# Small vectors on ScalarE's queue, router weights later, conv states in 96 partitions, and a query job ahead of the key norms

## The chip, the cores and the metric

The kernel runs on one core of a Trainium2 chip. The number that counts is the device time of one execution in microseconds (us). The core has a matrix engine (TensorE, here PE, with its weight loads PEld), a vector engine (VectorE, DVE), an activation engine (ScalarE, ACT), GpSimd (POOL) and SyncE (SP), which here only issues DMAs. Any of SP, ACT and POOL can issue a DMA; the profile calls these issues SPq, ACTq and POOLq.

## What is computed

One layer of a decoder trunk for a prompt of 256 tokens and 8 samples of one token each, 264 tokens in all, everything in float32:

```python
mod = jax.nn.silu(c) @ w['w_mod'] + w['b_mod']
h = rms_norm(x, w['g_norm1']) * (1 + sc1) + sh1
proj = h @ w['w_in']
q, k, v, fl, z, xbc, dtr, ga, gb = split_cols(proj, IN_SIZES)
q = rms_norm(q, w['g_q']);  k = rms_norm(k, w['g_k'])
logf = jax.nn.log_sigmoid(fl + w['b_f'])
o_att = forgetting_attention(...)      # adds the cumulated logf to the scores
xa = concat([conv0, xbc])              # conv0: 3 past columns per sample, 3072 channels
y_ssm = mamba2_branch(z, xbc, dt=softplus(dtr + dt_bias), a=-exp(a_log), d_skip, ...)
m = sigmoid(ga) * (o_att @ w_pa) + sigmoid(gb) * (y_ssm @ w_pb);  x += gt1 * (m @ w_o)
h2 = rms_norm(x, w['g_norm2']) * (1 + sc2) + sh2
x += gt2 * moe(h2)                     # router h2 @ w_router + b_router, 16 experts, 2 per token
```

## The kernel before

Activations lie transposed, features on the 128 partitions and the 264 tokens along the free axis, in eight blocks (KD). The work is a list of **jobs**, written out by hand at the start of `build`. Each engine's program walks the same list, and a job takes the next of seven PSUM banks in turn (`bank_of`). TensorE fills a bank, and ACT or DVE reads it out (`release`) and frees it with a semaphore. So the order of the list is the order of every engine's instructions. The first jobs are these:

- `cT` and `xt`: the condition and x are transposed on TensorE (`flip`, L1566).
- `vecs`: the vectors `vrow` are transposed. `ssq`: the sum of squares of x (L1603).
- `mod 1`, `modt 1`: the scale columns of the modulation (L1587, then two transposes). DVE then scales x (`normed`, L1120 to L1126).
- `cst 0`, `cst 1`: the conv states `csin` are transposed, 24 pieces of 24 x 128 (L1608), and DVE copies them to `stT` (L1201).
- `mod 0`, `modt 0`: the shift columns. DVE adds them for the samples (L1187, semaphore `h_samples`), and ACT adds them for the prompt, block after block (`shifted`, L846, semaphore `h_ready`).
- `fd`: dt and forget logits, eight matmuls with `w_forget_dt` (L1614). A long row of small DVE and ACT steps on `fd` follows.
- `k 0` to `k 3` (L1633) and `q 0` (L1629); `ft`: transposes of the head columns. It needs the end of the `fd` steps.
- `kn 0` to `kn 3` (L1636): sums of squares of the keys within a head. They need one DVE product of all four key blocks (L1254). ACT then takes four square roots (L897), DVE one reciprocal (L1258) and one scaling (L1260).
- `q 1` to `q 4`, `qn 0` to `qn 3` (the same four steps for queries 0 to 3), `q 5` to `q 7`, `v 0`, `qn 4` to `qn 7`, `v 1` to `v 3`. Then come attention, the Mamba branch, the merge, the router and the experts.

SP issues the weight slabs (1 MB each) in the order of use. There are six ring slots, and a slab goes out when the last job that read its slot has filled its bank. Two of the eight slabs of `mod 1` and `mod 0` lie in other tiles (`att_T`, `conv_out`). Between the last of those eight and the first input slab (the keys') SP runs `load_small`: two DMAs for `w_forget_dt`, one for the router's weights, and nine that put single floats onto partitions or one short row (g_q and g_k twice, dt_bias, b_f, a_log, d_skip, b_router). All twelve count on one semaphore, `late_in` (its name on the chip is small_weights_landed). TensorE waits for all twelve ahead of `fd`, and so does DVE. ACT issues the early loads: the conditions, x, the vectors of `vrow` with conv_w last, the conv states and the page table.

At the end SP streams the experts' weights in halves of 1 MB (L558) through 18 buffers, each released by TensorE.

## Time and profile before

| what | value |
|---|---|
| median of 3 runs | 831.83 us (828.68 to 833.68) |
| the profiled execution | 828.73 us |
| its span, first to last instruction | 827.1 us |
| TensorE busy | 768.6 us, 93% of the span |
| DVE, ACT, POOL busy | 365.9, 304.8, 95.4 us |
| DMA | 219.67 MB, 266 GB/s on the mean |

The profile shows one execution. Times of instructions are counted from the span's start. A row of the timeline has the start, the length, the engine, the line and the operation, and in brackets how long the engine had been idle before it and what the profile takes for the releaser. That releaser is inferred. Where the named engine had been done for long, something else released the wait. "PEclk" is the granted clock of TensorE as a share of full speed.

### The profile page before, as it was taken

What the parts mean: (1) busy time and instruction counts of PE and PEld (TensorE: products, weight loads), DVE (VectorE), ACT (ScalarE), POOL (GpSimd) and SP (SyncE); (2) the same over time, 40 slices, a digit from 0 to 9 for tenths busy, and PEclk for the clock granted to TensorE, in tenths of its full rate; (3) what the DMA queues carried; (4) which work ended last, traced back from release to release, by engine and by line L of the source; (5) the groups of instructions that cost most, each with busy time, mean ns of one, the idle gap of its engine ahead of it and who ended that gap; (6) DMA issues with size and microseconds to landing.
All of it is one profiled execution on the core that took longest, in us unless ns stands there. A gap on an engine that the chain in (4) does not pass through costs nothing.

```text
span 827.1 us, 12505 instructions
## 1 busy us (share of the span) xinstructions
PE 768.6 (93%) x4573; PEld 533.5 (64%) x4573; DVE 365.9 (44%) x847; ACT 304.8 (37%) x733; POOL 95.4 (12%) x156
## 2 busy tenths in 40 slices
PE   3798999999998999889999999999599999999997
PEld 3475787778776677679878788888343444344434
DVE  2455467777771373585998310122311133122213
ACT  1212247657763382646875001012221122122213
POOL 3321012112102105211111100000000000000000
PEclk9999999999999999999999989999689999999999
DMA  9797455969866323139998986353869999999992
GB/s 282 245 355 215 140 182 157 328 219 331 279 219 200 111 66 103 55 105 355 360 288 269 333 333 203 103 216 134 323 236 420 420 422 420 422 421 420 423 417 94
DMA packets 93531, 219.67 MB, mean 266 GB/s; under 512 B 11792, under 2 KB 67672, under 8 KB 78980
## 3 DMA queue, kind: packets, MB, share of 16 engines
q1 hardware_dynamic: 78850, 181.71, 60.3%
q0 software_dynamic: 7984, 31.87, 11.8%
q10 hardware_dynamic: 6634, 5.25, 2.0%
q8 instruction: 39, 0.64, 0.3%
q14 instruction: 24, 0.20, 0.1%
HBM read 207.58 MB, written 13.22 MB: 267 GB/s over the span
## 4 chain that ended last, share of the span: by engine, by line
PE 61%; DMA 12%; ACT 9%; DVE 6%; SPq 5%; issue 4%; POOL 1%; ACTq 1%; POOLq 1%; DVEq 0%
PE bank L1633 13%; PE bank L1943 9%; PE bank L1864 7%; SPq L558 5%; PE bank L1965 5%; PE bank L1566 4%; DMA out_ssm_sample<-arena 4%; PE bank L1629 4%; PE bank L1872 4%; DMA arena<-in_w_down 3%; PE bank L1846 3%; PE bank L1984 2%; PE bank L1587 2%; DMA arena<-in_conv_w 2%; DVE conv_work L1298 1%
## 5 line engine op out<-in xcount | busy, mean ns | idle before, releaser
L1633 PE MATMUL bank<-h_normed,weight_ring 128*128 128x264 f32 x1024 | 240.6, 392 | 4.4 <-ACT conv_work L998 2.0
L1633 PEld LDWEIGHTS bank<-h_normed,weight_ring 128*128 128x128 f32 x1024 | 193.6, 192 | 40.8 <-issue 3.5
L1943 PE MATMUL bank<-arena,h_normed 128*64 128x512 f32 x176 | 79.6, 607 | 0.0
L1864 PE MATMUL bank<-y_T,weight_ring 128*128 128x264 f32 x256 | 60.1, 399 | 0.2 <-DVE y_T L1412 0.2
L1943 PE MATMUL bank<-weight_ring,h_normed 128*64 128x512 f32 x192 | 56.3, 594 | 0.6 <-ACT h_normed L1040 0.6
L1864 PEld LDWEIGHTS bank<-y_T,weight_ring 128*128 128x128 f32 x256 | 50.4, 198 | 9.3 <-issue 0.3
L1492 DVE TENSOR_TENSOR arena<-arena,bank 128x512 f32<-128x512 f32 x8 | 8.8, 1098 | 105.0 <-PE bank L1943 105.0
L1499 DVE SCALAR_TENSOR_TENSOR x_residual<-bank,modulation,x_residual 128x256 f32<-128x256 f32 x64 | 28.8, 484 | 57.8 <-PE bank L1984 57.8
L1566 PE MATMUL bank<-identity,arena 128*128 128x128 f32 (+5 forms) x236 | 32.4, 279 | 15.5 <-ACT arena L839 9.4
L1566 PEld LDWEIGHTS bank<-identity,arena 128*128 128x128 f32 (+5 forms) x236 | 27.1, 150 | 26.1 <-issue 11.4
L990 ACT ACTIVATE arena<-conv_out,expanded 128x128 f32<-128x128 f32 x128 | 38.3, 388 | 11.2 <-DVE arena L1375 10.4
L1943 PEld LDWEIGHTS bank<-weight_ring,h_normed 128*64 128x64 f32 x192 | 17.5, 137 | 35.9 <-issue 34.8
L1040 ACT ACTIVATE h_normed<-bank,conv_tails 128x128 f32<-128x128 f32 x64 | 17.4, 382 | 60.8 <-PE bank L1566 60.8
L1965 PE MATMUL bank<-arena 128*64 128x512 f32 x88 | 39.2, 594 | 0.0
L1298 DVE SCALAR_TENSOR_TENSOR conv_work<-conv_work,vectors 128x288 f32<-128x288 f32 x72 | 37.5, 521 | 2.5
L808 POOL DMA_INDIRECT h_normed<-h_scratch,token_rows x8 | 8.1, 1010 | 264.8 <-DVE token_rows L1460 144.0
L1943 PEld LDWEIGHTS bank<-arena,h_normed 128*64 128x64 f32 x176 | 24.2, 140 | 13.8 <-issue 13.8
L1943 PE MATMUL bank<-conv_out,h_normed 128*64 128x512 f32 x64 | 30.6, 631 | 0.3 <-ACT h_normed L1040 0.3
L1872 PE MATMUL bank<-arena,weight_ring 128*128 128x264 f32 x128 | 30.2, 391 | 0.0
L1629 PE MATMUL bank<-h_normed,weight_ring 128*64 128x264 f32 x256 | 30.2, 397 | 0.0
L1984 PE MATMUL bank<-arena,conv_out 128*128 128x264 f32 x128 | 29.9, 387 | 0.0
L1846 PE MATMUL bank<-att_T,weight_ring 128*128 128x264 f32 x128 | 28.9, 387 | 0.0
(359 smaller groups left out, 1191.9 us busy)
## 6 DMA issues: line engine op xcount, KB each, us to landing
weight_ring<-in_w_in SPq DMA_DIRECT2D x36, 1024.0 KB, 5.9
weight_ring<-in_w_mod SPq DMA_DIRECT2D x22, 1024.0 KB, 9.8
arena<-in_w_up SPq DMA_DIRECT2D x14, 1024.0 KB, 19.9
weight_ring<-in_w_gate SPq DMA_DIRECT2D x14, 1024.0 KB, 19.9
arena<-in_w_down SPq DMA_DIRECT2D x11, 1024.0 KB, 26.3
weight_ring<-in_w_up SPq DMA_DIRECT2D x10, 1024.0 KB, 18.5
arena<-in_state_ssm POOLq DMA_DIRECT2D x8, 1024.0 KB, 8.8
out_ssm_sample<-arena POOLq DMA_DIRECT2D x8, 1024.0 KB, 9.7
```

What stands on the lines that cost most here:

```text
L558: sp.dma_start(half[s], (wg, wu, wdn)[kind][2 * j + e][:, 2048 * h:2048 * h + 2048]).then_inc(moe_full[s // 2], 16)
L990: ins = fn(bx[:, NST * c:NST * c + NST], bc[:, b, 0, :], ACT.Copy, scale=xdt[:, c, b:b + 1])
L1298: link(v.scalar_tensor_tensor(acc, x[:, w:w + XO], vec[:, 104 + 24 * w + i:105 + 24 * w + i], acc, ALU.mult, ALU.add), conv_ready if w == ...
L1566: return tr(out, x, ident[0:k, 0:k])
L1629: ins = mm(ps[64 * x:64 * x + 64, 0:T], slot(s)[:, c, o:o + HD], hT[:, c, :], start=c == 0, stop=c == KD - 1, tile_position=(0, 64 * x))
L1633: ins = mm(ps[:, 0:T], w, hT[:, c, :], start=c == 0, stop=c == KD - 1)
L1846: ins = mm(ps[:, 0:T], slot(s)[:, c, 128 * (i % 2):128 * (i % 2) + 128], attT[:, c, :], start=c == 0, stop=c == KD - 1)
L1864: ins = mm(ps[:, 0:T], w, yT[:, c, :], start=c == 0, stop=c == NXB - 1)
L1872: ins = mm(ps[:, 0:T], slot(s)[:, c, 128 * (i % 2):128 * (i % 2) + 128], gT[:, c, :], start=c == 0, stop=c == KD - 1)
L1943: ins = mm(banks[i][BLK * e:BLK * e + BLK, :], xg[:, 4 * h + c, BLK * e:BLK * e + BLK], ws[e][:, c, :], start=h == 0 and c == 0, stop=h == ...
L1965: ins = mm(banks[2 + q][BLK * e:BLK * e + BLK, :], aT[:, 2 * h + c, BLK * e:BLK * e + BLK], ws[e][:, c, 512 * q:512 * q + 512], start=h == ...
L1984: mm(comb_bank(c)[:, 0:T], outs[:, 128 * c:128 * c + 128], selT[:, j % 2, :], start=True, stop=True)\
```

## The change

Four edits. (1) The nine small DMAs leave SP's program for ACT's, behind the Silu of the conditions, and count on a semaphore of their own (`head_in`). TensorE's `fd` waits for the two weight DMAs only. DVE's first step on `fd` and ACT's Exp of a_log wait for `head_in`. (2) The router's weights are issued by SP four input slabs later, on a third semaphore. The router's first job `sw` waits for it. (3) The conv states are loaded as 96 rows of 768 floats in place of 24 rows of 3072. TensorE makes 6 transposes of 96 x 128 of them in place of 24, and DVE makes 6 copies of 96 elements with a stride in place of 2 copies of 288. (4) The job `q 1` stands ahead of `kn 0`.

```diff
-        csin = ar[:, D:D + CD]
+        csin = ar[0:96, D:D + CD // 4]
...
-        jobs += [("k", i) for i in range(4)] + [("q", 0)] + [("ft",)] + [("kn", i) for i in range(4)]
-        jobs += [("q", i) for i in range(1, 5)] + [("qn", i) for i in range(4)]
+        jobs += [("k", i) for i in range(4)] + [("q", 0), ("ft",), ("q", 1)] + [("kn", i) for i in range(4)]
+        jobs += [("q", i) for i in range(2, 5)] + [("qn", i) for i in range(4)]
...
-                sp.dma_start(wr[:], t["w_router"].rearrange("(k p) e -> p k e", p=128)).then_inc(late_in, 16)
-                for h in range(2):
-                    sp.dma_start(gqk[64 * h:64 * h + 64, 0:1], t["g_q"].rearrange("o d -> d o")).then_inc(late_in, 16)
...
+                if s == loads[loads.index(("in", COL_K)) + 4]:
+                    sp.dma_start(wr[:], t["w_router"].rearrange("(k p) e -> p k e", p=128)).then_inc(router_in, 16)
...
-            act.dma_start(csin[0:24, :], t["state_conv"].rearrange("o b w c -> (o b w) c")).then_inc(st_in, 16)
+            act.dma_start(csin, t["state_conv"].rearrange("o b w (q c) -> (o b w q) c", q=4)).then_inc(st_in, 16)
...
             link(fn(crow[0:NC, :], crow[0:NC, :], ACT.Silu), cond_ready)
+            for h in range(2):
+                act.dma_start(gqk[64 * h:64 * h + 64, 0:1], t["g_q"].rearrange("o d -> d o")).then_inc(head_in, 16)
...
                     link(fn(fdw[:, 0, :], fd[:], ACT.Abs))
+                    act.wait_ge(head_in, 16 * 9)
...
-                    release(dve, v.tensor_copy(stT[:, 12 * j[1]:12 * j[1] + 12, :],
-                                               ps[:, 0:288].rearrange("p (c s) -> p c s", c=12)), j)
+                    st4 = stT[:].rearrange("p (q c) s -> p c s q", q=4)
+                    for c in range(3):
+                        ins = v.tensor_copy(st4[:, 3 * j[1] + c], ps[:, 96 * c:96 * c + 96].rearrange("p (s q) -> p s q", q=4))
+                    release(dve, ins, j)
...
-                    for q in range(12):
-                        c = 12 * j[1] + q
-                        ins = flip(ps[:, 24 * q:24 * q + 24], csin[0:24, 128 * c:128 * c + 128])
+                    for q in range(3):
+                        c = 3 * j[1] + q
+                        ins = flip(ps[:, 96 * q:96 * q + 96], csin[:, 128 * c:128 * c + 128])
                 elif k == "fd":
-                    pe.wait_ge(late_in, 16 * 12)
+                    pe.wait_ge(late_in, 32)
...
                 elif k == "sw":
+                    pe.wait_ge(router_in, 16)
+                    pe.wait_ge(head_in, 16 * 9)
```

SP's issues between the last modulation slab and the sixth input slab, with what each waits for; before:

```order
L597 DMA conv_out<-in_w_mod 128x2x1024
L538 DMA w_forget_dt<-in_w_in 128x8x32
L539 DMA w_forget_dt<-in_w_in 128x8x16
L540 DMA w_router_sb<-in_w_router 128x8x16
L542 DMA qk_gain<-in_g_q 64x1
...
L548 DMA router_bias<-in_b_router 1x16
L599 DMA weight_ring<-in_w_in 128x8x256 [waits bank_filled2] x4
L599 DMA weight_ring<-in_w_in 128x8x256 [waits bank_filled6] x2
```

and after the change:

```order
L592 DMA conv_out<-in_w_mod 128x2x1024
L540 DMA w_forget_dt<-in_w_in 128x8x32
L541 DMA w_forget_dt<-in_w_in 128x8x16
L594 DMA weight_ring<-in_w_in 128x8x256 [waits bank_filled2] x4
L583 DMA w_router_sb<-in_w_router 128x8x16
L594 DMA weight_ring<-in_w_in 128x8x256 [waits bank_filled6] x2
```

The key slab follows the two weight DMAs at once, and the router's weights stand behind four slabs.

TensorE from the first query job to the first query norm, with bank waits, before (L1629 is a query job, L1636 a norm):

```order
L1566 MATMUL bank<-identity,head_work 128x32 x3
L1636 MATMUL bank<-conv_out,head_blocks 128x264 [waits qk_squared,bank_read1]
L1636 MATMUL bank<-conv_out,head_blocks 128x264 [waits qk_squared,bank_read2]
L1636 MATMUL bank<-conv_out,head_blocks 128x264 [waits qk_squared,bank_read3]
L1636 MATMUL bank<-conv_out,head_blocks 128x264 [waits qk_squared,bank_read4]
L1629 MATMUL bank<-h_normed,weight_ring 64x264 [waits slot_full2,bank_read5]
L1629 MATMUL bank<-h_normed,weight_ring 64x264 x15
```

and after (L1635 is a query job, L1642 a norm):

```order
L1572 MATMUL bank<-identity,head_work 128x32 x3
L1635 MATMUL bank<-h_normed,weight_ring 64x264 [waits slot_full2,bank_read1]
L1635 MATMUL bank<-h_normed,weight_ring 64x264 x15
L1642 MATMUL bank<-conv_out,head_blocks 128x264 [waits qk_squared,bank_read2]
L1642 MATMUL bank<-conv_out,head_blocks 128x264 [waits qk_squared,bank_read3]
L1642 MATMUL bank<-conv_out,head_blocks 128x264 [waits qk_squared,bank_read4]
L1642 MATMUL bank<-conv_out,head_blocks 128x264 [waits qk_squared,bank_read5]
```

The query job has moved in front of the four key norms, and three query jobs are left between them and the query norms.

ScalarE at the same place, before:

```order
L890 DMA out_logf_sample<-logf_tok 8x16
L897 ACT_TABLE_LOAD
L897 ACTIVATE conv_work<-bank1,eps_col 128x264 [waits bank_filled1]
L897 ACTIVATE conv_work<-bank2,eps_col 128x264 [waits bank_filled2,bank_read1]
```

and after:

```order
L894 DMA out_logf_sample<-logf_tok 8x16
L897 ACTIVATE arena<-bank 128x264 [waits bank_filled1]
L901 ACT_TABLE_LOAD [waits bank_filled2]
L901 ACTIVATE conv_work<-bank,eps_col 128x264 [waits bank_read1]
L901 ACTIVATE conv_work<-bank,eps_col 128x264 [waits bank_filled3,bank_read2]
```

The load of the square root's table waited for nothing before. Now it stands behind the wait for the first key norm's bank.

## Rows read from the trace of the kernel before

**Rows 1.** Section 1 of the page: busy time, share of the span, instructions.

```profile
PE 768.6 (93%) x4573; PEld 533.5 (64%) x4573; DVE 365.9 (44%) x847; ACT 304.8 (37%) x733; POOL 95.4 (12%) x156
```

**Rows 2.** Timeline of all engines, 11 to 59 us: start, length, instruction, idle before.

```profile
11.56 17.53 SPq L539 DMA_DIRECT2D w_forget_dt<-in_w_in  x1
...
24.70 1.28 ACT L868 ACT_TABLE_LOAD   x1 [15.49 <-issue]
...
29.14 3.94 SPq L540 DMA_DIRECT2D w_router_sb<-in_w_router  x1
...
33.12 0.60 SPq L542 DMA_DIRECT2D qk_gain<-in_g_q  x1
...
33.80 0.95 DVE L1201 COPY conv_states<-bank 128x288 f32<-128x288 f32 x2
...
35.12 0.41 PE L1566 MATMUL bank<-identity,mod_rows 128*128 128x128 f32 x2 [0.66 <-ACT mod_rows L865]
...
35.64 0.42 DVE L1176 TENSOR_TENSOR modulation<-bank,vectors 128x36 f32<-128x36 f32 x2 [0.89 <-PE bank L1566]
...
36.41 3.30 ACT L846 ACTIVATE h_normed<-conv_out,modulation 128x256 f32<-128x256 f32 x8 [1.43 <-DVE h_normed L1187]
...
37.69 0.32 SPq L548 DMA_DIRECT2D router_bias<-in_b_router  x1
...
38.95 5.42 PE L1614 MATMUL bank<-h_normed,w_forget_dt 128*48 128x264 f32 x16 [3.42 <-ACT h_normed L846]
...
44.30 14.51 PE L1633 MATMUL bank<-h_normed,weight_ring 128*128 128x264 f32 x64
```

**Rows 3.** Windows: bounds, length, busy of each engine, granted clock, DMA share, GB/s.

```profile
16.00:20.00 4.00, 3.37 (x18) 2.80 (x17) 3.57 (x10) 0.00 (x0) 0.00 (x0) 1.00 1.00 190
...
36.00:38.50 2.50, 0.00 (x0) 0.00 (x0) 0.29 (x2) 2.09 (x6) 1.06 (x2) 1.00 0.12 7
...
39.60:43.20 3.60, 3.60 (x10) 1.69 (x9) 0.00 (x0) 0.11 (x1) 1.51 (x3) 0.53 1.04 341
...
67.00:70.50 3.50, 3.50 (x16) 1.71 (x16) 1.51 (x1) 1.40 (x3) 0.00 (x0) 0.51 1.10 333
...
130.00:136.00 6.00, 5.98 (x42) 4.93 (x43) 4.97 (x13) 2.71 (x6) 0.96 (x2) 1.00 0.31 87
...
431.30:435.00 3.70, 3.69 (x11) 2.91 (x12) 3.70 (x4) 3.66 (x9) 0.71 (x2) 0.63 1.12 221
620.00:800.00 180.00, 178.28 (x858) 75.89 (x856) 39.92 (x109) 37.85 (x126) 5.95 (x6) 1.00 1.01 421
```

**Rows 4.** Timeline of all engines, 59 to 86 us.

```profile
58.84 3.86 SPq L599 DMA_DIRECT2D weight_ring<-in_w_in  x1
...
59.09 0.33 ACTq L878 DMA_DIRECT2D cf_scratch<-cums  x1
...
64.32 1.26 DVE L1254 TENSOR_TENSOR conv_out<-arena 128x1056 f32<-128x1056 f32 x1
...
64.93 1.28 ACT L897 ACT_TABLE_LOAD   x1 [1.27 <-DVE logf_tok L1243]
...
65.72 2.56 PE L1636 MATMUL bank<-conv_out,head_blocks 128*128 128x264 f32 x8 [2.48 <-DVE conv_out L1254]
...
68.21 15.55 PE L1629 MATMUL bank<-h_normed,weight_ring 128*64 128x264 f32 x128
...
68.99 6.75 DVE L1258 RECIPROCAL conv_work<-conv_work 128x1056 f32<-128x1056 f32 x1 [3.42 <-ACT conv_work L897]
...
83.70 2.05 PE L1636 MATMUL bank<-conv_out,head_blocks 128*128 128x264 f32 x8
```

**Rows 5.** Timeline of TensorE at two later idle times.

```profile
130.02 0.88 PE L1673 MATMUL bank<-arena 128*64 128x128 f32 x12 [1.34 <-ACT arena L913]
...
431.31 12.63 PE L1633 MATMUL bank<-h_normed,weight_ring 128*128 128x264 f32 x48 [1.97 <-ACT conv_work L998]
```

**Rows 6.** Waits of SP over the whole span: waiter, releaser, total us, times, longest.

```profile
SPq L558 <- PE bank L1943: 75.5, 21, 14.8
```

More of the change, by code:

```diff
@@ L353, in build @@
         st_in = sem("conv_states_landed")
-        late_in = sem("small_weights_landed")
+        late_in = sem("head_weights_landed")
+        head_in = sem("head_vectors_landed")
+        router_in = sem("router_weights_landed")
         pt_in = sem("page_table_landed")
@@ L539, in load_small @@
                 sp.dma_start(wfd[:, :, SH:HB], win[:, :, COL_F:COL_F + NH]).then_inc(late_in, 16)
-                sp.dma_start(wr[:], t["w_router"].rearrange("(k p) e -> p k e", p=128)).then_inc(late_in, 16)
-                for h in range(2):
-                    sp.dma_start(gqk[64 * h:64 * h + 64, 0:1], t["g_q"].rearrange("o d -> d o")).then_inc(late_in, 16)
-                    sp.dma_start(gqk[64 * h:64 * h + 64, 1:2], t["g_k"].rearrange("o d -> d o")).then_inc(late_in, 16)
-                sp.dma_start(hcol[0:SH, 0:1], t["dt_bias"].rearrange("o d -> d o")).then_inc(late_in, 16)
-                sp.dma_start(hcol[SH:HB, 0:1], t["b_f"].rearrange("o d -> d o")).then_inc(late_in, 16)
-                sp.dma_start(hcol[0:SH, 1:2], t["a_log"].rearrange("o d -> d o")).then_inc(late_in, 16)
-                sp.dma_start(hcol[0:SH, 2:3], t["d_skip"].rearrange("o d -> d o")).then_inc(late_in, 16)
-                sp.dma_start(brow[:], t["b_router"].rearrange("(o d) -> o d", o=1)).then_inc(late_in, 16)
             def states_stored(i):
@@ L839, in _ @@
             link(fn(crow[0:NC, :], crow[0:NC, :], ACT.Silu), cond_ready)
+            for h in range(2):
+                act.dma_start(gqk[64 * h:64 * h + 64, 0:1], t["g_q"].rearrange("o d -> d o")).then_inc(head_in, 16)
+                act.dma_start(gqk[64 * h:64 * h + 64, 1:2], t["g_k"].rearrange("o d -> d o")).then_inc(head_in, 16)
+            act.dma_start(hcol[0:SH, 0:1], t["dt_bias"].rearrange("o d -> d o")).then_inc(head_in, 16)
+            act.dma_start(hcol[SH:HB, 0:1], t["b_f"].rearrange("o d -> d o")).then_inc(head_in, 16)
+            act.dma_start(hcol[0:SH, 1:2], t["a_log"].rearrange("o d -> d o")).then_inc(head_in, 16)
+            act.dma_start(hcol[0:SH, 2:3], t["d_skip"].rearrange("o d -> d o")).then_inc(head_in, 16)
+            act.dma_start(brow[:], t["b_router"].rearrange("(o d) -> o d", o=1)).then_inc(head_in, 16)
             def shifted():
@@ L1200, in _ @@
                     ps = filled(dve, j)
-                    release(dve, v.tensor_copy(stT[:, 12 * j[1]:12 * j[1] + 12, :],
-                                               ps[:, 0:288].rearrange("p (c s) -> p c s", c=12)), j)
+                    st4 = stT[:].rearrange("p (q c) s -> p c s q", q=4)
+                    for c in range(3):
+                        ins = v.tensor_copy(st4[:, 3 * j[1] + c], ps[:, 96 * c:96 * c + 96].rearrange("p (s q) -> p s q", q=4))
+                    release(dve, ins, j)
                 elif k == "fd":
                     ps = filled(dve, j)
-                    dve.wait_ge(late_in, 16 * 12)
+                    dve.wait_ge(head_in, 16 * 9)
                     w0, w1, w2 = fdw[:, 0, :], fdw[:, 1, :], fdw[:, 2, :]
```

## The prediction

> **What bounds the kernel now.** The page's busy list comes first: TensorE is busy for 768.6 of 827.1 us, 93% [rows 1]. Nothing else is near that. So the end moves only if TensorE's idle time or its slow stretches shrink, and the reader should look for these at the places that the diff touches. Both are in the first 90 us. The timeline shows TensorE idle for 3.42 us ahead of the `fd` matmuls, and `fd` takes 5.42 us [rows 2]. It is idle for 2.48 us ahead of the key norms [rows 4]. The windows add that both gaps are followed by a slow stretch: from 39.6 to 43.2 us the granted clock was 0.53, from 67.0 to 70.5 us 0.51, that is, close to the lower of its two levels, 1.2 GHz in place of 2.4 [rows 3].
>
> **Who holds up `fd`.** The row names ACT's L846 as the releaser [rows 2]. I don't believe it. `fd`'s first matmul needs the first of ACT's eight blocks only. They start at 36.41 us and take 3.30 us together, 0.41 each, so the first was there at 36.82, and the matmul starts at 38.95, 2.1 us later. What else it waits for are the twelve DMAs of `load_small`. The first of the nine vectors was issued at 33.12 and the last at 37.69, done at 38.01, 0.9 us ahead of the matmul [rows 2]. In the stretch from 36 to 38.5 us the DMA engines moved 7 GB/s [rows 3]: they wait for issues, not for bytes. The cost is SP's, 4.9 us for nine issues one after another, and the key slab stands behind them.
>
> **Edit 1, the vectors on ACT's queue.** ACT has room: it was idle for 15.49 us before its table load at 24.70 [rows 2], so from 9.2. Nine issues at SP's pace end at 14.1, and nothing there waits for ACT. `fd` then needs the two weight DMAs and ACT's first block. The weight DMAs are in the queue by 29.09, when SP turns to the next issue [rows 2]; I take them as landed by 36, since from there on only those 7 GB/s moved [rows 3]. So `fd` starts at 36.82 plus a little, 36.9: **2.05 us gained**. The key slab is now issued from 29.1 on. The router's DMA needed 3.94 us for its issue in that place, so the slab may be in the queue at 33.1. In the trace the slab was used without an idle time at 44.30, at most 6.3 us after its issue at 38.05 [rows 2]. That puts it at 39.4 at the latest, and `fd` ends at 40.6 or later: covered, with 1.2 us to spare. ACT's and DVE's new waits for `head_in` stand where the old one stood on DVE, and behind the Abs on ACT. Their data are on the way 20 us earlier, so I cost them at nothing.
>
> **The clock in `fd`.** The slow stretch cost 3.6 us x (1 - 0.53) = 1.7 us [rows 3]. The idle time ahead of it shrinks from 3.42 to 36.9 - 35.53 = 1.4 us, with 0.66 us just before it, on the other side of two transposes [rows 2]. Two rows lie on either side: 1.34 us of idle at 130.02 left the clock at 1.00, and 1.97 us at 431.31 was followed by 0.63 [rows 3, 5]. 1.4 plus 0.66 lies between them, so I take half, **0.85 us**, with 0 and 1.7 as the ends.
>
> **Edit 3, conv states in 96 partitions.** On TensorE 24 transposes become 6, ahead of `mod 0`. This can bring at most what DVE leaves. DVE's copies start at 33.80 and the modulation's add at 35.64 [rows 2]. Two copies of 288 elements took 0.95 us and two operations of 36 elements 0.42 [rows 2], so a copy of 96 should take some 0.27 and six of them 1.6 us. They end at 35.4, before the add's 35.64. So nothing is lost, and at most 0.2 is gained. If the stride makes each copy as dear as one of 288, they end at 36.7 and `fd` starts 1.05 later: the low end of this term. I take 0.
>
> A rule bears on this edit. From 16 to 20 us the DMA engines are full and move only 190 GB/s, against 421 in the experts' stretch [rows 3]; this is where the conv states are on the way. The Trainium skill, page "SBUF — State Buffer", on the DMA port swizzle, says that partitions reach SBUF over 16 ports by some bits of their number, so that 24 partitions use six of them and 96 all. By that rule the full rate comes back there and the modulation's slabs land up to 2 us earlier. The sum would gain no more than the 0.2 us above, since DVE is next.
>
> **Edit 2, the router's weights.** They are first used some 430 us later, in `sw`. Their DMA now goes ahead of the fifth input slab, which waits for `mod 0` anyway. Nothing, unless that slab becomes late. It serves `q 4`, over 30 us on.
>
> **Edit 4, `q 1` ahead of the key norms.** Before: idle from 63.24 to 65.72, and a slow stretch that cost 3.5 x (1 - 0.51) = 1.7 us, of which 2.56 - 2.05 = 0.5 lies in the norms and 1.2 in the four query jobs behind (15.55 us, so 3.6 each at full clock) [rows 3, 4]. After: `q 1` runs from 63.24 to 66.85. The keys' product ended at 65.58 [rows 4], so the norms follow at once, until 68.9. Three query jobs last until 79.7, where before the query norms started at 83.70. But a new wait is due there. ACT's table load stood ahead of the norms' wait, at 64.93 [rows 4]. Now it stands behind the first norm. From the norms' start to the reciprocal it took 68.99 - 65.72 = 3.27 us; with the table's 1.28 added and the clock's 0.5 taken off, the reciprocal starts at 66.85 + 4.05 = 70.9 and ends at 77.65 (6.75 us). Scaling (1.3, as the product of equal size) ends at 78.95, the queries' product (1.26) and its signal at 80.35. TensorE waits for some 0.7 us, and **3.3 us are gained** (83.70 - 80.35). Later steps keep their distances.
>
> **Does it reach the end?** SP waits for TensorE's expert matmuls 21 times, 75.5 us in all [rows 6]. So the experts' stream is released by TensorE's progress, although it runs at 421 GB/s from 620 to 800 us [rows 3]. It starts earlier by what TensorE gains.
>
> **The sum.** 2.05 + 0.85 + 0 + 3.3 = 6.2 us. The profiled execution took 828.73 us (span 827.1, 1.6 around it), which gives 822.5. It lies 3.1 below the median of the runs shown, 831.83; the median is what will be compared, so the forecast is 831.83 - 6.2 = **825.6 us**. The ends of the terms (1.0 to 2.25, 0 to 1.7, 2.5 to 4.0) give gains of 3.5 to 8.0, so 823.8 to 828.3.
>
> **Rivals.**
> - *The vectors were not what held up `fd`.* The profile names ACT, and the sixth block ends near 38.9. Then `fd` stays where it is, and 3.3 us remain: 828.5. Against it: no instruction of TensorE waits for the sixth block there.
> - *The gap moves to the query norms.* If the chain over ACT and DVE is 2.5 us longer than I make it, edit 4 brings 0.8, and the sum is 3.7: 828.1. For it: the table load behind the wait; against: the rest of the chain has rows.
> - *The gain is lost downstream.* If the experts' stream had a start of its own, the end would not move: 831.8. The stream's full 421 GB/s speaks for it, SP's waits against.
> - *Slower: ACT's issues are held behind SP's.* SP's second weight DMA held its issue for 17.53 us, until 29.09 [rows 2]. If ACT's nine stand behind that, they end at 29.1 + 4.9 = 34.0, and the root behind them, due at 24.70, comes 9.3 us late. Less some 2 us of slack on DVE, `fd` starts at 44.1, 5.2 later than before; less the 3.3 of edit 4, the time is some 2 us up: 834. It decides from about 33 us on: until then the other gains cover the hold. Against it: at 59.09 ACT issued a DMA in 0.33 us, inside an issue of SP that was held for 3.86 [rows 4].
>
> The Trainium skill's page "DMA: Bandwidth & Descriptors" (Queues, rings and completion order) says that SP and ACT have rings of their own but no descriptor generator of their own, which leaves that rival open; its section "Issuing engines are not separate DMA queues" says that a second issuing engine saves issue time only. Issue time is what the rows show to be short.
>
> **Chances.** Forecast 0.60; vectors not the cause 0.12; gap moves 0.10; lost downstream 0.10; slower 0.08. About 0.5%, 4.2 us, is what a measurement can tell from no change. Below 827.7 lie most of the forecast's cases and a few of the second and third rival's: faster 0.60. Slower than 836 needs the last rival with more than its price, or a slab that comes late, and medians of a kernel whose runs spread over 5 us: 0.07. The rest, 0.33, is the same. The range takes in the forecast's own ends, spread by some 2 us, and the three rivals without a slowdown: 822 to 832.
>
> **What would show it.** Right: in the trace of after, `fd` starts within 0.2 us of ACT's first block; the idle time ahead of it is under 2 us; no idle time ahead of the key norms and a clock of 1.00 behind them; 0.3 to 1.2 us idle ahead of the query norms; every later landmark some 6 us earlier. Wrong: `fd` at or after 38.5; ACT issues of more than 1 us each; a wait for the key slab; DVE's copies past 35.6; an end that keeps its time while the start of the attention moves.

## The result

The changed kernel takes **824.86 us** (median of 11 runs, 822.07 to 828.33), the kernel before 829.92 (11 runs beside it, 828.68 to 833.68): ratio 0.9938, 95% interval [0.9917, 0.9958]. That is 5.1 us less, 0.6%; 825.6 was forecast. Two later measurements of the same kernel say that this was probably a lucky sample: 828.11 against 830.04, ratio 0.9980 [0.9954, 1.0007], and 827.38 against 829.55, ratio 0.9982 [0.9951, 1.0013]. Neither of the two can be told from no change by itself. The median of all 35 runs is 826.3. The kernel before, timed against itself, gave 829.53, ratio 1.0003 [0.9977, 1.0030]. So the gain is some 3.5 us, with single runs of either kernel spread over 10. The second median and that of edit 1 below each take in one slow execution, more than 1.5% above the kernel's fastest (834.61 and 836.80), which the ratios leave out; without it they are 827.72 and 826.49.

The profiled execution of the changed kernel took 828.33 us (span 826.8 against 827.1 before); it is the slowest of its 11. Its page, busy time of each engine (compare [rows 1]):

```profile
PE 767.7 (93%) x4555; PEld 530.6 (64%) x4555; DVE 365.6 (44%) x851; ACT 304.5 (37%) x733; POOL 95.6 (12%) x156
```

These sums show nothing of the change. The timeline of all engines from 9 to 46 us shows what the page doesn't (start, length, instruction, idle time before; compare [rows 2]):

```profile
9.33 0.54 ACTq L836 DMA_DIRECT2D qk_gain<-in_g_q  x1
...
11.62 15.37 SPq L541 DMA_DIRECT2D w_forget_dt<-in_w_in  x1
...
13.88 0.30 ACTq L842 DMA_DIRECT2D router_bias<-in_b_router  x1
14.28 1.28 ACT L871 ACT_TABLE_LOAD   x1 [4.97 <-issue]
...
27.03 8.76 SPq L594 DMA_DIRECT2D weight_ring<-in_w_in  x4
...
31.45 1.07 PE L1593 MATMUL bank<-conv_out,cond_T 128*32 128x256 f32 x16 [0.45 <-DMA conv_out<-in_w_mod]
...
32.31 1.33 DVE L1207 COPY conv_states<-bank 128x96 f32<-128x96 f32 x6
...
33.70 0.43 DVE L1180 TENSOR_TENSOR modulation<-bank,vectors 128x36 f32<-128x36 f32 x2
...
34.46 3.30 ACT L849 ACTIVATE h_normed<-conv_out,modulation 128x256 f32<-128x256 f32 x8 [1.43 <-DVE h_normed L1191]
35.12 5.42 PE L1620 MATMUL bank<-h_normed,w_forget_dt 128*48 128x264 f32 x16 [1.53 <-ACT h_normed L849]
```

ACT's nine issues end at 14.18, none held. `fd` starts 0.66 us after ACT's first block begins (0.41 for the block and a signal), at 35.12 in place of 38.95. The idle time ahead of it fell from 3.42 to 1.53 us, and yet `fd` takes 5.42 us as before: the windows show the granted clock low behind it again (columns as in [rows 3]):

```profile
32.00:34.00 2.00, 0.93 (x14) 0.24 (x6) 1.81 (x10) 0.38 (x1) 0.83 (x2) 1.00 0.98 333
34.00:36.00 2.00, 0.88 (x3) 0.44 (x4) 0.35 (x2) 1.54 (x4) 0.78 (x2) 0.79 1.11 337
36.00:38.00 2.00, 2.00 (x6) 0.98 (x5) 0.00 (x0) 1.76 (x5) 0.54 (x1) 0.50 1.11 336
```

The timeline from 54 to 92 us, all engines (compare [rows 4]):

```profile
59.33 3.78 PE L1635 MATMUL bank<-h_normed,weight_ring 128*64 128x264 f32 x32
...
63.04 2.05 PE L1642 MATMUL bank<-conv_out,head_blocks 128*128 128x264 f32 x8
63.16 0.39 ACT L897 ACTIVATE arena<-bank 128x264 f32<-128x264 f32 x1 [3.48 <-PE bank L1635]
63.84 1.28 ACT L901 ACT_TABLE_LOAD   x1 [0.29 <-PE bank L1642]
...
67.28 6.75 DVE L1264 RECIPROCAL conv_work<-conv_work 128x1056 f32<-128x1056 f32 x1 [5.54 <-ACT conv_work L901]
...
76.83 2.02 PE L1642 MATMUL bank<-conv_out,head_blocks 128*128 128x264 f32 x8 [0.91 <-DVE conv_out L1260]
```

`q 1` (59.33) fills the gap, the key norms (63.04) follow without an idle time and at full clock, and the wait that was forecast ahead of the query norms is there, 0.91 us. The query norms start at 76.83, 6.87 us before the old 83.70.

**Where the lead went.** The table gives the lead, in us, over the first profile of the kernel before: how much earlier the same instructions of all engines start (median over a stretch of 15 us that begins at the time given). Positive is earlier; "end" is the difference of the spans. The kernels under the first four rows are explained below. Every profile of this study stands in the table.

```
profile                  90    330    345    375    420    450    690   end
changed, first         6.90   7.03   5.76   7.39   0.93   1.11   0.37   0.4
changed, second        5.25   4.48   4.70   4.74   4.74   3.89   4.63   2.4
changed, third         5.72   3.71   3.23   4.86  -1.25  -1.07  -0.25  -0.9
before, second         0.33   0.82   0.83   0.83   0.83   0.65   0.10   0.0
edit 1 alone           1.61   1.62   3.31   3.31   3.31   3.20   3.44   3.1
edit 4 alone           2.61   2.97   2.97   2.97   2.97   1.50   2.73   2.3
edit 3 alone           2.20   2.47   2.47   2.47   1.79  -0.19  -0.16  -1.9
four small packets     1.25   1.30   1.54   1.58   0.99  -0.10   1.45   1.4
split semaphore       -0.58  -0.71   0.97   2.59  -3.09  -4.20  -3.43  -3.8
+ table load           5.36   5.11   4.60   6.23  -0.25  -0.08   0.89  -1.0
+ filler matmuls       7.73   3.81   3.93   3.94   3.94   1.11   3.85   3.8
+ stores on GpSimd     7.18   7.04   8.73  10.36  10.36   8.10   5.55   2.7
+ all three            9.69  10.23   9.53  11.15  11.15   9.27  12.05  11.5
```

A lead of 5.3 to 6.9 us leaves the first 90 us of the changed kernel, as the forecast said, and from 600 to 815 us any lead is carried on, within 0.5 us. In the first and the third profile it is lost between 375 and 420 us: 6.5 and 6.1 us, 1.6 of which had only just come from matmuls at full clock (345 to 375 us). ACT's queue shows where. Timeline of ACT in the first profile:

```profile
371.09 0.39 ACTq L974 DMA_DIRECT2D out_ssm_prompt<-arena  x1
372.25 0.60 ACT L973 ACTIVATE arena<-bank 128x512 f32<-128x512 f32 x1 [1.19 <-PE bank L1798]
372.88 7.09 ACTq L974 DMA_DIRECT2D out_ssm_prompt<-arena  x1
380.09 4.20 ACT L994 ACTIVATE arena<-conv_out,expanded 128x128 f32<-128x128 f32 x14 [7.25 <-issue]
```

and in the second, where the lead was kept:

```profile
373.74 0.39 ACTq L974 DMA_DIRECT2D out_ssm_prompt<-arena  x1
374.90 0.60 ACT L973 ACTIVATE arena<-bank 128x512 f32<-128x512 f32 x1 [1.19 <-PE bank L1798]
375.53 0.61 ACTq L974 DMA_DIRECT2D out_ssm_prompt<-arena  x1
376.26 4.78 ACT L994 ACTIVATE arena<-conv_out,expanded 128x128 f32<-128x128 f32 x16 [0.76 <-ACT arena L973]
```

The fourth store of the prompt's final states was held for 7.09 us on ACT's queue, and the products for the sample states (L994), which VectorE's chain waits for, stand behind it. The chain of work that leads to 421 us in the first profile runs through that issue:

```profile
372.88 7.09 ACTq L974
...
382.15 2.73 ACT arena L994 x9
...
384.91 1.28 DVE arena L1381
```

### The profile page after: what moved, and what is told of

Same layout as the page of the kernel before. It is cut to its first block, busy times and chain, and to the rows that moved or that the text cites. A ratio compares the mean times of both kernels' runs of the same rounds, so it can differ in the third digit from the quotient of the medians.

```text
span 826.8 us, 12475 instructions
## 1 busy us (share of the span) xinstructions
PE 767.7 (93%) x4555; PEld 530.6 (64%) x4555; DVE 365.6 (44%) x851; ACT 304.5 (37%) x733; POOL 95.6 (12%) x156
## 4 chain that ended last, share of the span: by engine, by line
PE 65%; DVE 11%; ACT 8%; DMA 6%; issue 4%; SPq 2%; ACTq 1%; POOL 1%; POOLq 1%; DVEq 0%
PE bank L1639 14%; PE bank L1951 11%; PE bank L1872 7%; PE bank L1973 6%; PE bank L1572 4%; PE bank L1880 4%; DMA arena<-in_w_down 3%; PE bank L1854 3%; PE bank L1992 3%; PE bank L1635 2%; DVE arena L1381 2%; SPq L551 2%; PE bank L1593 2%; DVE arena L1385 2%; DMA arena<-in_x_sample 1%
## 5 line engine op out<-in xcount | busy, mean ns | idle before, releaser
L994 ACT ACTIVATE arena<-conv_out,expanded 128x128 f32<-128x128 f32 x128 | 38.3, 388 | 17.5 <-DVE arena L1381 10.2
L1635 PE MATMUL bank<-h_normed,weight_ring 128*64 128x264 f32 x256 | 29.4, 388 | 0.0
## 6 DMA issues: line engine op xcount, KB each, us to landing
arena<-in_w_up SPq DMA_DIRECT2D x14, 1024.0 KB, 19.9
```

The source lines that it names most:

```text
L994: ins = fn(bx[:, NST * c:NST * c + NST], bc[:, b, 0, :], ACT.Copy, scale=xdt[:, c, b:b + 1])
L1635: ins = mm(ps[64 * x:64 * x + 64, 0:T], slot(s)[:, c, o:o + HD], hT[:, c, :], start=c == 0, stop=c == KD - 1, tile_position=(0, 64 * x))
```

## The experiments

**The changed kernel, unedited, twice.**

> The changed kernel once more, for a second profiled execution. My reading of the first pair of traces: the change is 3.8 us ahead at the start of fd, 6.9 us ahead at the end of the first query norms, 5.8 us ahead at the ssm_prompt products, and only 1.1 us ahead at the start of the pa jobs, because one DMA issue of ScalarE was held for 7.09 us there. Theory A (the hold is an accident of that execution): this trace has no such hold, and keeps 4 us or more of its lead up to the pa jobs; end near 824. Theory B (the hold comes with the change, since the stores meet SP's slabs 6 us earlier): it is here again, and the lead at the pa jobs is again under 2 us. The fast sum of squares (3.80 us against 5.52 before) should be the clock's state at the start and not the change: it may be here or not.

> The changed kernel once more, unedited. It had 824.9 and 828.1 us in two measurements, against 829.9 and 830.0 for the kernel before, and single edits 826.8 to 828.5. A third decides between a gain of 5 and one of 2: if the landmarks are right (7.0 and 4.5 us of lead at 330 us, less what the held store takes in some executions), 825 to 827. In its trace: fd starts within 0.3 us of ScalarE's first block, 0.9 us of idle ahead of the query norms, and a held fourth store only if the first store comes within 0.2 us of the state load.

Times above. In the second profile `fd` starts at 35.48 and takes 6.71 us, in the third at 36.29 and takes 5.42. Each stands behind 2.15 us of idle time, in place of 1.53: VectorE's six copies end 0.7 us behind the transposes there, and the modulation's add waits for them. This happens where the statistics' matmuls (`ssq`) took 5.07 and 5.49 us; in the first profile they took 3.80. These matmuls vary like that in every kernel of this study (the kernel before 5.52 and 5.36, edit 1 alone 3.80), so it isn't the change. In the third profile the trace has the clock at 0.50 from 19.8 to 23.2 us, in the others with long `ssq` matmuls at 1.00, so why is open. In the profiles with long `ssq` matmuls TensorE doesn't wait for the last modulation slab at all. What it gains there is the time of the conv states' transposes, 6 in place of 24: from the transposes of `modt 1` to the first matmul of `mod 0` it takes 0.84 us in the changed kernel's third profile, in place of 1.94. Before, then after:

```profile
28.87 0.41 PE L1566 MATMUL bank<-identity,mod_rows 128*128 128x128 f32 x2 [0.66 <-ACT mod_rows L865]
...
30.81 1.93 PE L1587 MATMUL bank<-weight_ring,cond_T 128*32 128x256 f32 x32
```

```profile
28.57 0.41 PE L1572 MATMUL bank<-identity,mod_rows 128*128 128x128 f32 x2 [0.66 <-ACT mod_rows L868]
...
29.41 1.93 PE L1593 MATMUL bank<-weight_ring,cond_T 128*32 128x256 f32 x32
```

The 0.91 us of idle time ahead of the query norms is there in all three. In the second profile the fourth store isn't held (0.61 us), so the hold doesn't come with the change each time. In the third profile the fourth store is held again, 6.74 us, with the first store 0.11 us after the state load, as expected.

**The kernel before, unedited.**

> The kernel before, unedited, as a measure of what time and trace do by themselves. Time 829 to 830.5. In its trace fd starts 0.9 to 1.0 us after the last vector's issue ends, 1.5 us or more after ScalarE's first block; the last modulation slab is used between 32.8 and 33.4 us however fast the statistics' matmuls were; and its landmarks lie within 2 us of those of the first look.

829.53 us. Its instructions start within 0.9 us of those of the first profile. `fd` starts at 38.63, 2.76 us after ACT's first block begins and 1.28 after the last vector's issue (0.9 to 1.0 expected). The timeline of this profile names the releaser rightly, `router_bias`, the last vector; the first profile's named ACT. The last modulation slab is used at 32.86.

**Edit 1 alone** (the nine vectors by ACT; the router's weights stay in place).

```
-                sp.dma_start(gqk[...], t["g_q"]...).then_inc(late_in, 16)   # and eight more
+            act.dma_start(gqk[...], t["g_q"]...).then_inc(head_in, 16)      # and eight more
```

> The kernel before with edit 1 alone: the nine vector DMAs on ScalarE's queue, TensorE's fd waits for the two weight DMAs only, the router's weights stay in place on SP with a semaphore of their own. Theory (the vector issues held fd and the key slab): fd starts within 0.2 us of ScalarE's first block, near 36.9 where the sum of squares runs as before, with an idle time ahead of it of about 1.4 us; the later jobs are about 2 us ahead, the time is 2 to 4 us below the kernel before. Rival (ScalarE held fd, as the profile names it): fd starts at the end of the sixth block, 2.5 us after the first, and nothing is gained. Second rival: the key slab, still behind the router's weights, comes late and fd's gain turns into a wait ahead of the keys.

827.32 us, ratio 0.9961 [0.9932, 0.9990]. TensorE's timeline:

```profile
33.23 1.94 PE L1590 MATMUL bank<-conv_out,cond_T 128*32 128x256 f32 x16 [2.05 <-DMA conv_out<-in_w_mod]
35.82 0.66 PE L1569 MATMUL bank<-identity,mod_rows 128*128 128x128 f32 x2 [0.66 <-ACT mod_rows L867]
38.00 6.40 PE L1617 MATMUL bank<-h_normed,w_forget_dt 128*48 128x264 f32 x16 [1.53 <-ACT h_normed L848]
```

The idle time ahead of `fd` is down to 1.53, as in the changed kernel. But the chain ahead of it starts from the last modulation slab, which is used at 33.23, and its matmuls ran at half the clock (1.94 us, not 1.07). Without that slow stretch `fd` would have started at 37.1, close to the 36.9 that I had worked out for this edit. The other 1.8 us of the changed kernel's first profile must come from elsewhere.

**Edit 3 alone** (conv states in 96 partitions).

```
-            act.dma_start(csin[0:24, :], t["state_conv"].rearrange("o b w c -> (o b w) c")).then_inc(st_in, 16)
+            act.dma_start(csin, t["state_conv"].rearrange("o b w (q c) -> (o b w q) c", q=4)).then_inc(st_in, 16)
```

> The kernel before with edit 3 alone: conv states in 96 partitions. Theory (DVE comes next and fd is held by the vectors on SP anyway): fd starts at 38.9 less at most 0.3, time unchanged within 1 us; the DMA rate from 16 to 20 us goes up from 190 to over 300 GB/s, and the last modulation slab lands about 2 us earlier. The issue of SP's second weight DMA, 17.53 us before, ends about 2 us earlier, and with it the row of vector issues behind it: if that is so, fd starts up to 2 us earlier and the edit gains 2 us by that way. Both are told apart by the start of the first vector issue (33.1 before) and by fd's start.

828.49 us, ratio 0.9972 [0.9950, 0.9993]. `fd` starts at 36.29, 2.66 us earlier than in the first profile of the kernel before and 2.34 earlier than in its second, though it still waits for the vectors: everything on SP's queue is earlier, the second of the two ways that were expected. SP's second weight DMA is held for 15.17 us, not 17.53, and the last modulation slab is used at 30.75. The DMA engines move 342 GB/s from 16 to 20 us, against 190 in [rows 3]:

```profile
16.00:20.00 4.00, 3.12 (x20) 2.41 (x20) 3.74 (x11) 0.00 (x0) 0.00 (x0) 1.00 1.02 342
```

**Which property of the load does it: partitions or packets?** The kernel before, with the conv states still in 24 partitions but by four DMAs, so that a row's packet has 3,072 bytes as in the 96-partition form, not 12,288.

```
-            act.dma_start(csin[0:24, :], t["state_conv"]...).then_inc(st_in, 16)
+            for q in range(4):
+                act.dma_start(csin[0:24, q * CD // 4:(q + 1) * CD // 4], t["state_conv"]...).then_inc(st_in, 16)
```

> The kernel before, with the conv states loaded by four DMAs instead of one: still 24 partitions, but rows of 3,072 bytes in place of 12,288, the size that the 96-partition form has. It tells apart what gave edit 3 its gain. In the two kernels with 24 partitions the DMA engines moved 185 to 217 GB/s from 16 to 20 us and SP's second weight DMA was held for 17.5 and 18.0 us; with 96 partitions they moved 307 to 376 and it was held for 15.2. Theory A, the number of partitions that are written limits the rate: 185 to 220 GB/s again and a hold of 17.5 to 18 us, the last modulation slab used at about 33.1. Theory B, the large packets do it: over 300 GB/s, a hold of 15 to 15.5 us, the slab used near 31. Three more issues on ScalarE's queue cost 1 to 2 us where it has room.

827.31 us in a single run. From 16 to 20 us:

```profile
16.00:20.00 4.00, 3.34 (x21) 2.63 (x20) 3.73 (x10) 0.00 (x0) 0.00 (x0) 1.00 1.03 285
```

The result lies between the two theories. The trace's packets, averaged while the conv states are on the way:

```
profile              its packets      mean ns   bytes per ns   others' 4,096 B, ns   MB moved by 22 us
before               24 of 12,288 B     954         12.9             316                   6.41
before, second       24 of 12,288 B     916         13.4             308                   6.62
24 partitions x 4    96 of  3,072 B     175         17.6             231                   6.96
edit 3 alone         96 of  3,072 B     162         19.0             204                   7.29
changed, first       96 of  3,072 B     158         19.5             208                   7.14
```

The other queue's packets take 170 ns from 10 to 12 us and 163 from 22 us on. So the long packets into few partitions slow everybody's. Cutting them brings more than half of the bytes back, writing to 96 partitions the rest. What the kernel gets of it is less, some two fifths: the slab is used at 32.24, against 33.13 and 33.23 with edits 4 and 1 alone, where TensorE waited for it too, and 30.75 with edit 3; `fd` starts at 37.71, against 38.63 and 38.95, and 36.29. SP's hold, 17.24 us, lies among those of the kernels with long packets (16.96 to 18.38). The three additional issues on ACT end the load later (its last packet starts at 19.9 us, at 18.1 with edit 3), so the shares aren't exact.

**Edit 4 alone** (`q 1` ahead of the key norms).

```
-        jobs += [("k", i) for i in range(4)] + [("q", 0)] + [("ft",)] + [("kn", i) for i in range(4)]
+        jobs += [("k", i) for i in range(4)] + [("q", 0), ("ft",), ("q", 1)] + [("kn", i) for i in range(4)]
```

> The kernel before with edit 4 alone: q 1 ahead of the key norms. Theory: no idle time ahead of the key norms, no slow stretch behind them, 0.7 to 0.9 us idle ahead of the first query norms, and from the start of ft to the start of those norms 18 us in place of 21.3: 3.3 us gained. Time 2 to 3.5 us below the kernel before. Rival (what is gained there is lost again later, at the states of the samples): the lead of 3.3 us at the norms is under 1 us at the pa jobs, and the time is the same.

826.78 us, ratio 0.9979 [0.9955, 1.0004]. From the start of the keys to that of the query norms it takes 36.36 us (44.75 to 81.11), against 39.40 before: 3.04 us. With edit 1 alone, where no slow stretch followed the 2.48-us gap, the same distance was 37.75. So 1.4 us of the gain is the gap, and 1.65 the clock, which goes down behind this gap in some executions only.

**Is it the vectors' landing that `fd` waits for?** The kernel before; `fd` waits for its two weight DMAs alone. The vectors and the router's weights count on semaphores of their own, and no DMA is moved.

```
-                    pe.wait_ge(late_in, 16 * 12)
+                    pe.wait_ge(late_in, 32)
```

> The kernel before with one change: fd waits for its two weight DMAs only; the vectors and the router's weights keep their places on SP's queue and get semaphores of their own, on which VectorE, ScalarE and the router stage wait. If the vectors' issues hold fd (my reading), fd starts at 36.9 to 37.2, within 0.3 us of ScalarE's first block, with some 1.4 us of idle ahead of it in place of 3.3; VectorE's part of fd is not late, since the vectors are in by 39 and fd ends after 41. The keys' slab is still issued from 38.0 on, as before, so the keys gain at most what the slab allows: start between 42.3 and 44.3. Rival, ScalarE's blocks or the weight DMAs hold fd: it starts at 38.6 to 39.0 as before.

832.52 us in a single run. TensorE's timeline:

```profile
36.58 3.73 PE L1617 MATMUL bank<-h_normed,w_forget_dt 128*48 128x264 f32 x16 [1.53 <-ACT h_normed L848]
43.60 17.43 PE L1636 MATMUL bank<-h_normed,weight_ring 128*128 128x264 f32 x64 [3.29 <-DMA weight_ring<-in_w_in]
```

`fd` starts 0.66 us after ACT's first block, with 1.53 us of idle: the wait for the vectors was the cause. And it gains nothing: the keys' slab, issued behind the vectors at 37.37, is late now. TensorE waits 3.29 us for it and then runs the keys at a lower clock, 17.43 us in place of 14.51. The wait was only a part of the vectors' cost, SP's 4.9 us of issues the other; moving them takes both away. It also bears on the clock: 1.53 us of idle time, and `fd` ran at full speed (3.73).

**Three additions to the changed kernel.** First, ACT's table load ahead of `q 1`'s copy:

```
+                    if j == ("q", 1):
+                        fn(rw[7][:, 0:1], epsc[:], ACT.Sqrt)
```

> The changed kernel, plus a square root of one column on ScalarE ahead of its copy of q 1, so that the table load stands before the wait for the key norms and not behind it. If the load is what makes TensorE wait ahead of the query norms (0.91 us of idle in both looks at the changed kernel), the roots start 1.28 us earlier after the key norms, that idle time is gone, and the query norms start 0.9 us earlier counted from the start of the keys (36.37 us before, 35.5 here). Rival, VectorE's 6.75-us reciprocal and product set it by themselves from another start: the wait stays at 0.5 us or more. On the whole time 0.9 us, which can't be told.

824.22 us, ratio 0.9931 [0.9905, 0.9957]. ACT's and TensorE's timeline:

```profile
63.59 1.28 ACT L898 ACT_TABLE_LOAD   x1 [1.33 <-DVE logf_tok L1251]
...
66.33 2.02 ACT L903 ACTIVATE conv_work<-bank,eps_col 128x264 f32<-128x264 f32 x4 [0.21 <-PE bank L1644]
```

```profile
65.53 2.05 PE L1644 MATMUL bank<-conv_out,head_blocks 128*128 128x264 f32 x8
67.50 10.90 PE L1637 MATMUL bank<-h_normed,weight_ring 128*64 128x264 f32 x96
78.33 2.05 PE L1644 MATMUL bank<-conv_out,head_blocks 128*128 128x264 f32 x8
```

There is no idle time ahead of the query norms, and they start 35.38 us after the keys: as expected.

Second, filler matmuls in the idle times ahead of `fd`, whose results nobody reads (two more stand ahead of the modulation's last transposes):

```
+                    for _ in range(5):
+                        mm(sbank[:, 0:128], onesf[:], onesf[:], start=True, stop=True)
                     pe.wait_ge(late_in, 32)
```

> The changed kernel, plus seven matmuls of 128x128 on data that nobody reads: two ahead of the last two transposes of the modulation and five ahead of fd, in TensorE's idle times there. If the idle time ahead of fd is what lowers the clock, it is 1.00 from 33 to 43 us and fd takes 3.7 us, against 5.42 and 6.71 in the two looks at the changed kernel: 1.7 to 3.0 us earlier at the start of the keys, counted from the start of fd. Rival, the low stretch has another cause or comes with the slab's wait: fd takes over 5 us still. On the whole time 1.7 to 3 us, at the edge of what can be told.

825.32 us, ratio 0.9939 [0.9909, 0.9969]. `fd` takes 3.73 us and the clock stays at 1.00:

```profile
33.59 1.28 PE L1620 MATMUL bank<-ones 128*128 128x128 f32 x10
35.98 3.73 PE L1625 MATMUL bank<-h_normed,w_forget_dt 128*48 128x264 f32 x16 [1.11 <-ACT h_normed L849]
```

Filling the idle time kept the clock up, here and in the kernel with all three additions; in the five profiles of the changed kernel without the filler (three unedited, one with the table load, one with the stores on GpSimd), `fd` ran at the low level in part. Idle time by itself doesn't decide it, as the split semaphore shows. In this profile a low stretch of 10 us, from 247.2 on, took 3.7 us back (lead 7.16 at 240 us, 3.42 at 275), at idle times of under 1 us that the other kernels have too. The changed kernel's third profile has one of 3.4 us there, from 248.5 on, so it needs no filler.

Third, the four state stores issued by GpSimd instead of ACT:

```
-                    act.dma_start(fs_d[0, :, 4 * i:4 * i + 4, :], ...).then_inc(o_fs, 16)
+            for i in range(4):
+                read_out(pool, ("fs", i))
+                pool.dma_start(fs_d[0, :, 4 * i:4 * i + 4, :], ...).then_inc(o_fs, 16)
...
+                        act.wait_ge(o_tail, 16 * 12)
```

The last line is a wait of ACT, at a later sigmoid, for the stores of the conv states.

> The changed kernel, with the four stores of the prompt's final states issued by GpSimd instead of ScalarE. In the looks so far ScalarE's fourth store was held for 7.1 to 7.6 us in three (the changed kernel's first look among them), where its first store came 0.1 us after GpSimd's state load, and for 0.4 to 2.5 us in seven, where it came 1.5 to 1.7 us after. In the three, 4 to 6 us of lead were lost between 372 and 450 us. Theory: the held issue costs that lead, since ScalarE's products for the sample states stand behind it. Then here ScalarE begins them within 1 us of its copy of the fourth group, whatever the clock did, and the lead over the kernel before at 450 us is within 1.5 us of that at 345. On the median time up to 2 us less than the changed kernel's, with a narrower spread. Rival: GpSimd's issue is held in its place, and the state loads or the B and C vectors behind it come late: the same loss under another name, or more.

824.37 us, ratio 0.9938 [0.9909, 0.9967], 3.0 us under the changed kernel measured beside it. GpSimd's timeline:

```profile
364.50 0.54 POOL L763 DMA_DIRECT2D arena<-in_state_ssm  x1
369.55 1.05 POOL L763 DMA_DIRECT2D arena<-in_state_ssm  x2 [4.50 <-PE bank L1801]
370.59 3.02 POOL L778 DMA_DIRECT2D out_ssm_prompt<-arena  x4
```

Its four issues take 3.02 us and aren't held; ACT's products begin at 369.97, right behind its fourth copy at 369.34. The lead is 10.36 at 375 and at 420 us, and 8.10 at 450, against 8.73 at 345: kept, up to the next low stretches of the clock. 2.6 us more of it went in the router's stage, where the clock was low for 30.7 us from 570.7 on (20.5 from 585.9 in the kernel before).

When is the store held? With ACT issuing, the time from GpSimd's state load to ACT's first store, and how long the fourth was held:

```
profile              gap us   held us        profile           gap us   held us
changed, first        0.11     7.09          before, first         1.62     0.63
changed, third        0.11     6.74          before, second        1.53     0.62
+ table load          0.10     7.08          changed, second       1.67     0.61
split semaphore       0.11     7.55          edit 1, edit 4        1.46, 1.58   0.39, 0.78
                                             edit 3, 4 packets     1.65, 1.64   2.31, 2.45
                                             + filler matmuls      1.72     0.39
```

A gap of 0.1 us goes with a hold of about 7 us in four of four, a gap of 1.5 to 1.7 with one of at most 2.45 in eight. In the eight, the final-state matmuls just before fell into a low stretch of the clock (in the kernel before 370.8 to 374.2); in the four they ran at full clock and were 1.6 us faster.

What a hold costs is read from 375 to 420 us in the table. The four with some 7 us lost 5.7 to 6.5 us of lead there, the two with 2.3 and 2.45 us lost 0.7 and 0.6, and all others, the two with GpSimd's issues among them, lost nothing. From 420 us on leads move with low stretches of the clock (with the filler matmuls 3.94 at 420, 1.11 at 450, with such a stretch from 445.2 on). Why the queue holds the store I can't show, only when.

**All three together.**

> The changed kernel with all three additions: table load ahead of q 1's copy, the seven matmuls in idle time ahead of fd, GpSimd's issue of the state stores. If their gains are separate, the start of the query norms is 0.9 us earlier counted from the keys, fd takes 3.7 us, no issue of ScalarE is held over 1 us near 375 us, and the time is 2 to 4 us under the changed kernel's, about 822. Rival: the low stretches of the clock that follow elsewhere, and the 10-us one that the kernel with the seven matmuls had at 247 us, eat what was gained: 824 to 826.

**818.77 us** (6 runs, 817.36 to 824.08), ratio 0.9888 [0.9851, 0.9924] to the kernel before, and 8.6 us under the changed kernel measured beside it. TensorE's timeline:

```profile
34.96 3.73 PE L1630 MATMUL bank<-h_normed,w_forget_dt 128*48 128x264 f32 x16 [0.61 <-ACT h_normed L853]
38.62 14.51 PE L1649 MATMUL bank<-h_normed,weight_ring 128*128 128x264 f32 x64
```

More than the 2 to 4 us expected. The lead of 9.7 us at 90 us is 1.7 from `fd` and 0.9 from the table load above the changed kernel's first profile, and 1.8 us more are there at the end: nothing is lost on the way for good. The profiled execution is the fastest of the kernel's six. How much of the rest is the luck of the clock's stretches one profile can't tell.

## Why the prediction was right

The time, 824.86 us, is within 0.8 us of the forecast, and the kernel came out faster in that measurement, though in neither of the two repeats by more than their intervals. The steps did less well than the sum, and part of the hit is luck. The forecast took 6.2 us off 831.83, the median of three runs; over 11 runs the kernel before has 829.92. From there the same gain would have given 823.7. The gain itself was 5.1 us, and some 3.5 over all runs, for 6.2.

- **Who holds up `fd`: right.** The split semaphore shows it, and in the five profiles in which the wait is on SP's vectors `fd` starts 0.94 to 1.28 us after their last issue's end.
- **Edit 1: right in size.** Forecast 36.9 for `fd`; 37.1 by edit 1 alone, once its slow matmuls are put back to full clock. The key slab and ACT's room were as forecast: issues of 0.30 to 0.62 us, no wait for the slab. The rival in which ACT's issues are held behind SP's is out: they went through while SP's second weight DMA was held for 15.37 us. Two of the signs that were named missed: `fd` starts 0.66 us after ACT's first block starts (0.25 after its end), where 0.2 was named, and the idle time ahead of it is 2.15 us in two of three profiles, where under 2 was.
- **Edit 3 at nothing: wrong.** It is worth 2.3 to 2.7 us at `fd` alone, and beside edit 1 what lies between the forecast's 36.9 and the measured 35.12, 35.48 and 36.29, so 0.6 to 1.8. The step that failed was "this can bring at most what DVE leaves", with an add at 35.64 that I took as fixed. The add waits for the modulation's last transposes ([rows 2] has 0.89 us of idle ahead of it), and these moved. Where `ssq` is short, they wait for the last modulation slab, and that came some 2 us earlier: it was used, after a wait, at 33.13 and 33.23 with edits 4 and 1 alone, and at 30.75 to 31.45 in the four such profiles with the new load. Where `ssq` is long, TensorE doesn't wait for the slab. There the six transposes save it 1.1 us, and VectorE's copies take 0.6 of that back, which is not far from the forecast's 0.2. The copies cost 0.22 each (0.27 forecast). The row that told of the slab was cited, 190 GB/s in [rows 3]. The Trainium skill's page "SBUF — State Buffer" (the DMA port swizzle) led to the right size, 2 us, by a mechanism that carries only a part of it: packets of a quarter the length into the same 24 partitions gave more than half of the bytes back, and some two fifths of what `fd` gained.
- **The clock, 0.85 us: wrong size, 0 or less.** `fd` took 5.42, 6.71 and 5.42 us, against 5.42 before, so the term brought 0, -1.3 and 0. I took half, a mean of two levels, with 0 as the lower end; the second profile lies below it. The same 1.53 us of idle time was followed by a low stretch in the changed kernel and by none in the split one, so interpolating between two rows by the length of the idle time could not give this term.
- **Edit 4, 3.3 us: right.** 3.0 us were measured, and the new wait 0.91 us for 0.7. From the key norms' start to the reciprocal 4.24 us (4.05 forecast), from there to the query norms 9.55 (9.45).
- **Does it reach the end: half right.** From 600 to 815 us all leads are carried within 0.5 us. "Later steps keep their distances" failed at the state stores, where 6.5 and 6.1 us are lost in two of three profiles. In these two the end hardly moves, 0.4 and -0.9 us, while the leads at 90 us are 6.9 and 5.7: one of the prediction's own signs of being wrong. The rival "lost downstream" named the experts' stream as its place; the place was an issue queue 250 us earlier. So 5.3 to 6.9 us were gained by 90 us, and some 3.5 kept in the medians.

So the sum is near the measurement because errors cancel: 0.6 to 1.8 us too little for edit 3, 0.85 us or more too much for the clock, no loss at the stores, and a starting value 1.9 us too high.

## What to carry over

When issues block a queue, count both who waits for what they bring and what stands behind them; taking away only the wait moves the stall to the next slab. The time at which a transfer lands isn't fixed: ask which transfers run beside it and whether a neighbour's long packets into few partitions slow them. Where an engine both computes and issues stores, a gain upstream can turn into a held issue; move such stores to an engine with nothing urgent behind them, and read several profiles before a gain of 1% is believed. Compare two kernels at several points of the span: one late number hides what was gained and lost on the way.

## What the hardware showed unexpectedly

- 24 packets of 12,288 bytes took 0.92 to 0.95 us each, and 4,096-byte packets on another queue beside them 308 to 316 ns, 163 later on.
- Matmuls that ran 1.6 us faster, and with them a gap of 0.1 us in place of 1.5 to 1.7 between two engines' issues, went with a store's issue held for 7 us, and 5.7 to 6.5 us of lead lost.
- Seven matmuls on unused data, 2 us of TensorE's work in its idle time, kept the clock at 2.4 GHz and went with 3.73 us for `fd`, in both profiles that have them, in place of 5.40 to 6.71 in the five without.
- The same 1.53 us of idle time ahead of `fd` was followed by a low clock in some kernels and not in another; 2.48 us ahead of the key norms likewise (2.02 us for the norms with edit 1 alone, 2.56 and 2.95 for the kernel before).
